# The embedding's product moved from the feed-forward stage to the start of a hybrid transformer layer, through memory

## The reference, cut to what matters

```
h   = layer_norm(x, ln_in_g, ln_in_b)
mix = hybrid_mixer(h, ...)                  # retention, gated delta rule, LRU, output product
h   = layer_norm(DN_ALPHA * h + mix, ln1_g, ln1_b)
ffn = moe(h, ...)                           # 64 experts, 8 per token, and one shared expert
ple = sigmoid(h @ ple_w_g + ple_b_g) * (p @ ple_w_e)      # p (1024, 256), ple_w_e (256, 1024)
out = layer_norm(DN_ALPHA * h + ffn + ple, ln2_g, ln2_b)
```

## Time and profile before

| what | value |
|---|---|
| median of 3 runs | 2537.09 us (2535.78 to 2537.4) |
| the profiled execution's own time | 2537.53 us |
| its span | 2535.4 us, 26796 instructions |
| mean granted clock of TensorE | 0.988 |
| PE matmul busy | 2438.1 us (96%), weight load 1478.4 us |
| DVE, ACT, POOL busy | 893.0, 437.6, 805.6 us |
| DMA | 391.37 MB, mean 154 GB/s |

### The profile page before, as it was taken

The page is one execution under the profiler, slowest core; times in us unless marked ns, Lnnn a source line. Parts: engine busy times, 40 slices in busy tenths (PEclk is TensorE's granted clock), DMA queues, the critical chain, the costliest instruction groups (busy, mean ns, idle before and its releaser), DMA issues. The chain is left out here.

```text
span 2535.4 us, 26796 instructions
## 1 busy us (share of the span) xinstructions
PE 2438.1 (96%) x10446; PEld 1478.4 (58%) x10446; DVE 893.0 (35%) x1522; ACT 437.6 (17%) x689; POOL 805.6 (32%) x764
## 2 busy tenths in 40 slices
PE   6999999999999999999999999999999999999992
PEld 3444554344699644444444544467777777787761
DVE  5010564575533523323223352222222223332224
ACT  1001122434454100100100110001111111111112
POOL 3000111011253100000001115436676666766654
PEclk9999999999999999999999999999999999999996
DMA  6201003100000211111142231269999999999995
GB/s 252 91 33 36 32 34 105 42 17 9 1 1 26 92 50 36 39 50 44 32 148 77 98 131 50 79 250 348 343 342 347 349 343 343 346 343 343 347 349 176
DMA packets 168141, 391.37 MB, mean 154 GB/s; under 512 B 19882, under 2 KB 40410, under 8 KB 167248
## 3 DMA queue, kind: packets, MB, share of 16 engines
q1 hardware_dynamic: 135424, 300.64, 32.6%
q0 software_dynamic: 31584, 82.00, 12.5%
q10 hardware_dynamic: 1008, 7.02, 0.7%
HBM read 322.50 MB, written 67.11 MB: 154 GB/s over the span
## 5 line engine op out<-in xcount | busy, mean ns | idle before, releaser
L1876 PEld LDWEIGHTS banks<-arena 128*128 128x128 f32 x4096 | 520.4, 191 | 58.0 <-issue 33.7
L1876 PE MATMUL banks<-arena 128*128 128x128 f32 (+7 forms) x4096 | 530.0, 290 | 13.5 <-DMA arena<-in_exp_w_gu 11.2
L2311 POOL DMA_INDIRECT arena<-hp_scratch,arena x306 | 295.0, 964 | 223.1 <-issue 80.0
L1380 PE MATMUL banks<-arena 128*128 128x512 f32 x672 | 293.4, 597 | 1.3 <-PEq L736 1.3
L328 PE MATMUL banks<-arena 128*128 128x512 f32 x640 | 280.9, 596 | 4.6 <-DVE arena L1093 4.3
L1884 PE MATMUL banks<-arena 128*128 128x512 f32 (+1 forms) x528 | 237.3, 592 | 1.3 <-DVE arena L2270 0.9
L1380 PEld LDWEIGHTS banks<-arena 128*128 128x128 f32 x672 | 128.3, 191 | 164.1 <-issue 163.9
L328 PEld LDWEIGHTS banks<-arena 128*128 128x128 f32 x640 | 120.0, 190 | 159.4 <-issue 149.7
L280 POOL TENSOR_SCALAR arena<-arena 128x1 f32<-128x1 f32 x16 | 15.5, 971 | 606.7 <-DVE arena L271 606.7
L2326 POOL DMA_INDIRECT acc_scratch<-arena x99 | 153.7, 1552 | 67.4 <-DMA acc_scratch<-arena 43.0
L321 PE MATMUL banks<-arena 128*128 128x512 f32 x384 | 168.1, 596 | 0.6 <-PE banks L321 0.6
(11 more groups left out here) (372 smaller groups left out, 2453.2 us busy)
## 6 DMA issues: line engine op xcount, KB each, us to landing
arena<-in_exp_w_gu SPq DMA_DIRECT2D x64, 2048.0 KB, 24.4
arena<-in_exp_w_down SPq DMA_DIRECT2D x64, 1024.0 KB, 20.5
arena<-in_w_in SPq DMA_DIRECT2D x10, 2048.0 KB, 9.0
arena<-in_w_in SPq DMA_DIRECT2D x12, 1024.0 KB, 6.1
arena<-in_w_branch SPq DMA_DIRECT2D x12, 512.0 KB, 7.1
hp_scratch<-arena SPq DMA_DIRECT2D x10, 512.0 KB, 2.7
acc_scratch<-arena SPq DMA_DIRECT2D x10, 512.0 KB, 4.0
arena<-hp_scratch,arena POOLq DMA_INDIRECT x306
```

Source lines behind the costliest of these rows:

```text
L1380: last = nc.tensor.matmul(PS[:, g % 4, :], lhs[:, k, :], rhs[:, k, :], start=(k == 0), stop=(k == 3))
L1876: last = nc.tensor.matmul(PS[:, bank + part, f * n:(f + 1) * n], weights[:, k, part * FF + f * P:part * FF + (f + 1) * P], x[:, k, 0:n], s ...
L2311: nc.gpsimd.indirect_dma_start(out=rows[0:n, :], out_offset=None, in_=table, in_offset=bass.IndirectOffsetOnAxis(ap=at, axis=0)).then_inc( ...
```

## The change

The product `p @ ple_w_e` is computed at the start of the first stage. SP loads `p` and `ple_w_e` ahead of x. TensorE turns `p` and makes the 16 pieces in banks 2 and 3 before its first `turn_tile`; ScalarE copies them into 16 buffers of SBUF. 13 of these lie in space that the retention uses later; three more, `p` and the weights lie where k and v will be written, so that VectorE waits for the stores before it evacuates job 8. SP stores the 16 pieces (256 KB each) into a new HBM tensor behind `h_scratch`. In the last stage the transposes and the product are gone; ScalarE's queue fetches the pieces into four buffers, four ahead at first and then one behind each sigmoid, three pieces ahead; VectorE multiplies by them from SBUF. The two loads of 1 MB leave that stage. SLOTS_AT goes from 9 to 12. `f_pl` counts one per piece instead of two.

```diff
-SLOTS_AT = 9
+SLOTS_AT = 12
...
+        e_d = nc.dram_tensor("embed_scratch", (P, NT, D), F32).ap()
...
+        take = lay(base + NT * W, base + 3 * NT * W)
+        p_in = take(NT * PLE).rearrange("p (t n) -> p t n", t=NT)
+        p_T = take(2 * SEQ).rearrange("p (f s) -> p f s", f=2)
+        p_we = take(2 * D).rearrange("p (f n) -> p f n", f=2)
+        p_out = [carve(HALF, R_RING + 2 * KD * W + 3 * W + i * HALF) for i in range(13)] + [take(HALF) for _ in range(3)]
...
             def _(sp):
+                sp.dma_start(p_in, a["p"].rearrange("(t p) n -> p t n", p=P)).then_inc(b_p, 16)
+                sp.dma_start(p_we, a["ple_w_e"].rearrange("(f p) n -> p f n", p=P)).then_inc(b_we, 16)
                 for i in range(2):
                     sp.dma_start(h[:, 2 * i:2 * i + 2, :], xv[:, 2 * i:2 * i + 2, :]).then_inc(a_x[i], 16)
...
                 sp.dma_start(h_d, h).then_inc(h_saved, 16)
+                sp.wait_ge(b_ev, 2 * NT)
+                for q in range(2 * NT):
+                    t, j = q // 2, q % 2
+                    sp.dma_start(e_d[:, t, j * HALF:(j + 1) * HALF], p_out[q]).then_inc(b_st, 16)
                 for g in range(2, 6):
...
                 pe.wait_ge(a_id, 16)
+                pe.wait_ge(b_p, 16)
+                for i in range(NT // 2):
+                    if i >= 2:
+                        pe.wait_ge(b_pT, i - 1)
+                    for c in range(4):
+                        last = nc.tensor.transpose(PS[:, 2 + i % 2, c * P:(c + 1) * P], p_in[:, 2 * i + c // 2, c % 2 * P:(c % 2 + 1) * P], ident)
+                    last.then_inc(b_tp, 1)
+                pe.wait_ge(b_we, 16)
+                pe.wait_ge(b_pT, NT // 2)
+                for q in range(2 * NT):
+                    t, j = q // 2, q % 2
+                    if q >= 2:
+                        pe.wait_ge(b_ev, q - 1)
+                    for f in range(2):
+                        last = nc.tensor.matmul(PS[:, 2 + q % 2, :], p_T[:, f, t * P:(t + 1) * P], p_we[:, f, j * HALF:(j + 1) * HALF],
+                                                start=(f == 0), stop=(f == 1))
+                    last.then_inc(b_em, 1)
                 turn_tile(0)
...
+                pe.wait_ge(b_ev, 2 * NT)
                 tile_in(0)
...
             def _(act):
...
+                for i in range(NT // 2):
+                    act.wait_ge(b_tp, i + 1)
+                    nc.scalar.activation(p_T[:, :, 2 * i * P:(2 * i + 2) * P].rearrange("p f (t s) -> p t f s", t=2),
+                                         PS[:, 2 + i % 2, :].rearrange("p (t f s) -> p t f s", t=2, f=2),
+                                         ACT.Copy).then_inc(b_pT, 1)
+                for q in range(2 * NT):
+                    act.wait_ge(b_em, q + 1)
+                    nc.scalar.activation(p_out[q], PS[:, 2 + q % 2, :], ACT.Copy).then_inc(b_ev, 1)
...
                 for job in range(NT - 3, 24):
+                    if job == NT:
+                        v.wait_ge(b_pT, NT // 2)
+                        v.wait_ge(b_em, 2 * NT)
+                        v.wait_ge(b_st, 32 * NT)
                     evacuate(job)
```

And in the last stage:

```diff
-                sp.dma_start(pt, a["p"].rearrange("(t p) n -> p t n", p=P)).then_inc(f_p, 16)
...
-                sp.wait_ge(f_hid, 4)
-                sp.dma_start(we, a["ple_w_e"].rearrange("(f p) n -> p f n", p=P)).then_inc(f_we, 16)
...
                     elif r == 1:
+                        sp.wait_ge(f_pl, NT)
+                    elif r < RING:
                         sp.wait_ge(f_pl, 2 * NT)
-                    elif r < RING:
-                        sp.wait_ge(f_pl, 4 * NT)
...
-                pe.wait_ge(f_p, 16)
-                pe.wait_ge(f_up, 3)
-                for t in range(0, NT, 2):
-                    if t >= 4:
-                        pe.wait_ge(f_pT, t // 2 - 1)
-                    for c in range(4):
-                        tt, f = t + c // 2, c % 2
-                        last = nc.tensor.transpose(PS[:, 4 + (t // 2) % 2, c * P:(c + 1) * P], pt[:, tt, f * P:(f + 1) * P], ident)
-                    last.then_inc(f_tp, 1)
...
-                    last.then_inc(f_pl, 1)
-                    if q == 0:
-                        pe.wait_ge(f_we, 16)
-                    for f in range(2):
-                        last = nc.tensor.matmul(PS[:, 4 + q % 2, :], pT[:, f, t * P:(t + 1) * P], we[:, f, j * HALF:(j + 1) * HALF],
-                                                start=(f == 0), stop=(f == 1))
                     last.then_inc(f_pl, 1)
                     if q == SLOTS_AT:
...
-                for i in range(NT // 2):
-                    act.wait_ge(f_tp, i + 1)
-                    nc.scalar.activation(pT[...], PS[:, 4 + i % 2, :]..., ACT.Copy).then_inc(f_pT, 1)
+                def embedded(q):
+                    j, t = q // NT, q % NT
+                    act.dma_start(em[q % 4], e_d[:, t, j * HALF:(j + 1) * HALF]).then_inc(f_em[q % 4], 16)
+
+                act.wait_ge(o_job, 2 * NT)
+                for q in range(4):
+                    embedded(q)
                 for q in range(2 * NT):
                     act.wait_ge(f_lg, q + 1)
                     nc.scalar.activation(pg[q % 2], pg[q % 2], ACT.Sigmoid).then_inc(f_sg, 1)
+                    if 1 <= q <= 2 * NT - 4:
+                        act.wait_ge(f_pr, q)
+                        embedded(q + 3)
...
-                    v.wait_ge(f_pl, 2 * q + 2)
+                    v.wait_ge(f_em[q % 4], 16 * (q // 4 + 1))
                     v.wait_ge(f_sg, q + 1)
-                    link(nc.vector.tensor_tensor(pg[q % 2], pg[q % 2], PS[:, 4 + q % 2, :], ALU.mult))
+                    link(nc.vector.tensor_tensor(pg[q % 2], pg[q % 2], em[q % 4], ALU.mult))
```

More of the change, by code:

```diff
@@ L303, in build @@
         a_id, a_gb, a_par, a_x, a_chain = sem("a_ident"), sem("a_gb"), sem("a_params"), [sem(f"a_x{i}") for i in range(4)], sem("a_chain")
+        b_p, b_we, b_tp, b_pT, b_em, b_ev = (sem("b_" + n) for n in ("p", "we", "tp", "pT", "em", "ev"))
+        b_st = sem("b_st")
         a_zero, a_pad = sem("a_zero"), sem("a_pad")
@@ L1526, in build @@
         slot_q = carve(4 * P, R2 + 2 * D + NT * 15)
-        we = carve(2 * D, R2).rearrange("p (f n) -> p f n", f=2)
         up = [carve(HALF, R2 + i * HALF) for i in range(2)]
@@ L1535, in build @@
         hid = take(2 * SEQ).rearrange("p (f s) -> p f s", f=2)
-        pt = take(NT * PLE).rearrange("p (t n) -> p t n", t=NT)
-        pT = take(2 * SEQ).rearrange("p (f s) -> p f s", f=2)
+        take(NT * PLE)
+        em = [take(HALF) for _ in range(4)]
         bg_row = take(D)
@@ L1577, in build @@
         e_slots = [sem(f"e_slots{i}") for i in range(2)]
-        f_w, f_p, f_bg, f_wg, f_we = (sem("f_" + n) for n in ("w", "p", "bg", "wg", "we"))
-        f_gu, f_sl, f_up, f_hid, f_dn, f_acc, f_tp, f_pT, f_pl, f_lg, f_sg, f_pr, f_chain, f_sl2, f_slq, f_stp, f_int = (
-            sem("f_" + n) for n in ("gu", "sl", "up", "hid", "dn", "acc", "tp", "pT", "pl", "lg", "sg", "pr", "chain",
+        f_w, f_bg, f_wg = (sem("f_" + n) for n in ("w", "bg", "wg"))
+        f_em = [sem(f"f_em{i}") for i in range(4)]
+        f_gu, f_sl, f_up, f_hid, f_dn, f_acc, f_pl, f_lg, f_sg, f_pr, f_chain, f_sl2, f_slq, f_stp, f_int = (
+            sem("f_" + n) for n in ("gu", "sl", "up", "hid", "dn", "acc", "pl", "lg", "sg", "pr", "chain",
                                     "slots_in", "slots_quad", "slots_t", "slots_int"))
@@ L1843, in _ @@
                     last.then_inc(f_dn, 1)
-                pe.wait_ge(f_pT, 4)
                 for q in range(2 * NT):
@@ L1983, in _ @@
                     nc.scalar.activation(up[q % 2], PS[:, 5 + 2 * (q % 2), :], ACT.Copy).then_inc(f_up, 1)
-                for i in range(NT // 2):
-                    act.wait_ge(f_tp, i + 1)
-                    nc.scalar.activation(pT[:, :, 2 * i * P:(2 * i + 2) * P].rearrange("p f (t s) -> p t f s", t=2),
-                                         PS[:, 4 + i % 2, :].rearrange("p (t f s) -> p t f s", t=2, f=2),
-                                         ACT.Copy).then_inc(f_pT, 1)
+                def embedded(q):
[4 more added lines that the diff above has]
+                    embedded(q)
                 for q in range(2 * NT):
@@ L2168, in ple_logits @@
                     j = q // NT
-                    v.wait_ge(f_pl, 2 * q + 1)
+                    v.wait_ge(f_pl, q + 1)
                     if q >= 2:
@@ L2243, in _ @@
                 gates_in(0)
-                v.wait_ge(f_pl, 4 * NT)
+                v.wait_ge(f_pl, 2 * NT)
                 for r in range(NS):
```

## The result

The kernel after takes **2542.12 us** (median of 20 runs, 2536.73 to 2550.31). The kernel before, in 20 runs beside them, takes 2537.31 (2535.78 to 2542.67). The ratio is 1.0021, with 1.0015 to 1.0026 as its interval: slower by 4.8 us, close to what can be told from no change, where I had forecast 4.4 us of gain. 2542.12 is outside my range. The profiled execution of after took 2542.1 us, its span 2540.2, which is 4.8 more than the 2535.4 of before. So the two profiles show the whole difference.

The account below looks back on a forecast made before the run. TensorE was taken to set the pace up to 2143 us, SP's weight queue behind it. Start +18.2 and last stage -22.6 gave -4.4 against 2537.53: 2533.1, as median 2532.7, with a range of 2526.5 to 2538.5.

Parts of the forecast that it names:

- The start: First stage: loads, transposes and product ahead of the first job cost 18.2 us, with bounds of 15.8 and 21.4.
- the slow clock: Start of TensorE's program: its rise from 1.2 to 2.4 GHz costs 1.0 us, 2.7 at most.
- The slots: Last stage: GpSimd's copy ends at 1622.0, set by 64 scatters; with SLOTS_AT 12 TensorE comes at 1629.2 without waiting.
- the fetches, costed at nothing: Loop of the last stage: 256 KB fetches on ACT's queue, three pieces (20 us) ahead, delay nothing but the next sigmoid.
- L1841's place and length: Last stage, shared expert's second product: without the transposes it can start at 1512.3 instead of 1512.85, gaining 0.55 us.
- wait ahead of `hidden(1)`: Last stage: place 1's gathers are ready at 1664.1, `hidden(0)` ends at 1660.4, so TensorE newly waits 3.7 us.
- The dear start: Rival: `p` at 8.5 and all of the slow clock (21.4 us), or later gathers: -1.2 to +1.9 us; chance 0.15.
- The stores: Start, SP's queue: 16 stores of 256 KB land at about 103, before VectorE's job 8 at 110.6; no wait.
- The rival of late stores: Stores of 2.7 us one after the other land at 134.5, TensorE stands 17 us before job 10: 2550; chance 0.06.
- The loop: Last stage: 16 pieces lose 1.72 us each, 27.5 us; pieces last 6.88, with VectorE and ScalarE under 3.5 us.
- what TensorE gains at 1680 is handed on whole: Experts: TensorE gives the pace up to 2143 and the weights follow, so its gain at 1680 passes on in full.
- the weights lead: Rival, experts: loads waiting for the loop's last matmul start 28.0 us earlier and set the end, gaining 9.8: 2527.3; chance 0.2.

Follow-up runs that it names:

- consts_late: Kernel after with ACT's 1.67 MB of constants issued behind the four copies of turned `p` instead of ahead; ratio 1.0003 to the kernel before.
- combined: Kernel after with ACT's constants issued behind the copies of `p` and slot indices made before the next piece's bias; 2534.04 us, ratio 0.9985.
- half8: Kernel after with only pieces 0 to 7 computed at the start, the rest in the loop, constants late, indices first, SLOTS_AT 11; 2532.05 us, ratio 0.9978.
- change_again: Kernel after, unedited, run on the second chip; 2538.85 us, ratio 1.0010 to the kernel before.
- no_fetch_again: Kernel after without the fetches of pieces 4 to 15, first four buffers reused, on the second chip; 2538.34 us, ratio 1.0005.
- late_alone: Kernel before's first stage with the change's last stage, fetches reading pieces of x and no embedding computed; 2614.85 us on the slower chip, ratio 0.996.
- no_fetch: Kernel after without the fetches of pieces 4 to 15, first four buffers reused; 2629.51 us on the slower chip, ratio 1.003.
- index_first: Kernel after with VectorE turning slots into indices before it waits for the next piece's bias; 2537.08 us, ratio 0.9999.
- start_alone: Kernel before plus the change's start (loads, product, stores, VectorE's waits), last stage unchanged; 2647.19 us on the slower chip, ratio 1.0095.
- quarter4: Kernel after with four pieces at the start, twelve in the loop, constants late, indices first, SLOTS_AT 10; 2531.68 us, ratio 0.9979.
- before_fetch: Kernel before plus sixteen unused 256 KB fetches of x on ACT's queue and VectorE's waits for them; 2548.14 us, ratio 1.0043.

## Why the prediction was wrong

Two steps failed. The start was mis-sized: 23.7 us instead of 18.2, since the weights were there at 16.3 and not by 11.9, `p` at 9.4 and not at 7.0, and the slow clock cost 2.5 us and not 1.0. The slots were taken to be out of reach of the change: the fetches, costed at nothing, made the scatters 8.8 us longer, and TensorE stood 2.80 us. Falls of the clock added 3.4 us that no term held.

Forecast: behind `hidden(1)` 4.4 us earlier. Measured: 7.3 later. The 11.7 us between them, in the order of time (the 25.8 us of 15 embeddings are the same on both sides):

| step | forecast | measured | difference |
|---|---|---|---|
| start, at the first bias | +18.2 | +23.66 | 5.5 |
| on the way to GpSimd's last shared product | 0 | -0.5 | -0.5 |
| L1841's place and length | -0.55 | +1.3 | 1.9 |
| wait at the slots | 0 | 2.80 | 2.8 |
| small pieces to `hidden(0)` | 0 | 0.2 | 0.2 |
| wait ahead of `hidden(1)` | 3.7 | 3.9 | 0.2 |
| its clock | 0 | 1.67 | 1.7 |

The fourth row holds the copy's delay; the measured value of the sixth is 1692.34 less the 7.14 us of `hidden(0)` and its start. The sum is 11.8, with rounding.

**The start** failed by its terms and not by its mechanism. "Its landing took 6.3 us in the last stage ...: 7.0 here" was priced by a row in which little else flowed. Here it was 9.38, even past my bound of 8.5. "The weights ... are there by 11.9 even if they only start then" was the worse step: they took 15.0 us and TensorE stood 3.19. For `p` I had sharing with ACT's queue as a bound, for the weights I had left it out; ACT's queue loads its constants at the same time, and in consts_late and combined, which move them back, the transposes start 2.4 us earlier and the first job 4.3 and 4.8. How much of `p`'s 2.4 us is the constants' is open, since half8 has them late too and got `p` at 8.83. The clock was 2.5 us instead of 1.0, near the 2.7 that I had as the most. The dear start that I gave as a rival, 21.4, was still 2.3 too cheap.

**The stores** were right: in time, no wait at job 8, and "I cost them at nothing" held, with 2 us of margin where the forecast had 7.6 (103 against 110.6). The rival of late stores, by which each would take 2.7 us one after the other, is refuted: sixteen were issued in 19.32 us and each landed after 8.6, so they overlap. By the Trainium skill, "DMA: Bandwidth & Descriptors", section on the anatomy of one DMA, 2.0 us plus bytes over 436 GB/s would be 2.6 us for each. The page states this for DMAs that GpSimd issues, and the stores are SP's; here they took 8.6 one beside another, and some 28 us for all instead of 42.

**L1841** was to gain 0.55 and lost 1.3. Its start gained 0.5 as forecast. But TensorE now stands 1.79 us for GpSimd, where the transposes of `p` had kept it busy, and the clock fell in the product behind it: 29.43 us for the same 64 matmuls. Eight traces have this wait, of 1.78 or 1.79 us: in five the product lasts 29.43 (after, consts_late, change_again, combined, no_fetch_again), in three 27.73 (late_alone, no_fetch, index_first). So a fall is not certain; what decides is open.

**The loop** was right: VectorE's biases are 6.88 us apart, and the 27.5 us are gone from it. VectorE and ScalarE had the time, and every fetch landed before its piece.

**The slots** were the step that failed by its mechanism: "GpSimd's copy of the slots ends at 1622.0, set by 64 scatters and not by TensorE". True, but not set by the scatters' count alone. The 256 KB fetches of ScalarE's queue run beside them and make the landings later. None of them, or only the first four: 97.8 to 100.9 us (before, start_alone, no_fetch twice). All sixteen, of which ten are issued while the scatters of after run: 106.9 to 113.7 in the six traces with the change's last stage. Half8 with eight has 106.6. Quarter4 has 104.3 with the first four alone, where no_fetch had 98.8 and 100.9; so some 4 us of these differences are not explained by the number of fetches. before_fetch shows that they suffice (109.6, TensorE 7.00 us), no_fetch that the lengthening goes with them (100.9, and 98.8 when repeated). I had costed the fetches by whether *they* were in time; whom they delay I had not asked. That they take engines or a queue from the scatters, and which, no run tells apart.

**The wait ahead of `hidden(1)`** was right in size and cause: 3.66 us against 3.7, and in change_again 2.27 plus the 1.6 by which a slow `hidden(0)` shortened it, for gathers that hang on piece 13. no_fetch_again keeps it, index_first takes it away. That 1.7 us of slow clock would come with it I had not seen; in change_again they fell into `hidden(0)`.

**The experts.** TensorE does lead, longer than before. But "what TensorE gains at 1680 is handed on whole" is only half true. In the table, with both marks equal (half8, quarter4, before_fetch), the last load follows them within 0.8 us. Where they differ, it comes out between them (index_first lies 0.3 beside): after has 0.0 and 7.3 and gets 4.0. Behind that load the span of no_fetch_again comes out 3.4 us better than its mark, which is not explained. The weights' stream, which starts when the loop ends, carries part of the time; the rival "the weights lead" had that part right. By it alone after would have had no loss at 2441. By the Trainium skill, the same page, section Specifications, the limit is about 358 GB/s; the experts run at 345 and 346 whether TensorE leads or the weights, and on the other chip at about 315, so the rate doesn't tell who leads. Nor is 358 a limit that every stretch here keeps: 415 GB/s flowed from 9.40 to 16.30 in after.

Why medians follow the spans only in part (half8: -9.9 us in the profile, -4.5 in the median; index_first -2.0 and +0.6) is in part open: the profiled executions of these two and of combined lie at the lower end of their runs, that of quarter4 (2531.68) is its median. Part of the spread goes with the clock: the three fastest executions of half8 (2527.33 to 2527.7) have a mean granted clock of 0.988, the other eight 0.986 or 0.987. I take the ratios as the measure and the profile for the places.

## What to carry to other kernels

Work moved into an idle stretch costs nothing only up to where the next stage could have started; here some 14 of 27.5 us nearly fitted (4.3 us paid), and half of the product moved brought `hidden(0)` 10.3 us forward, the whole with the same repairs 5.0. The medians of the two do not separate; against the whole as first written (ratio 1.0010) half is better clear of noise (0.9978). A transfer that is itself always in time is not free: look for the chain of small DMAs beside it, and for the other queues that load in the same microseconds. When a due time (`SLOTS_AT`) is shifted, look at what stands behind it in program order on the engine that delivers it: two lines exchanged on VectorE brought the gathers 7.0 us closer to the slots and took a wait of 2 to 4 us away.

## What the runs showed of the hardware

- Sixteen plain loads of 256 KB on ScalarE's queue, eight of them issued while it ran, made a chain of 64 small indirect scatters of GpSimd about 10 us longer (99.8 to 109.6 us in before_fetch). In after, 71 and 38 GB/s flow in the two slices of the page that hold the chain.
- TensorE's granted clock fell to 0.50 for about three microseconds after it had stood for only 1.79 or 3.66 us, and cost 1.7 us each. It fell behind the wait of 1.78 or 1.79 us in five of eight traces, and within `hidden(0)`, behind a wait of 2.03, in change_again; behind its wait of 2.27 it did not fall.
- 1 MB loads of the start landed after 8.5 and 15.0 us beside ACT's constants, and after 6.2 and 10.8 with these behind them (combined). In half8, which has them late too, the first took 8.0.
- On one of two chips the same kernel took 2621.94 us instead of 2537, all of it in the experts as far as start_alone's marks tell (`hidden(0)` at 1701.55, where the start's 22 us put it). In the profiles of late_alone, no_fetch and consts_late there `hidden(0)` was broken by gaps of 0.4 to 1.8 us at single matmuls, some 6.3 us in all, that nothing in the profile explains. In start_alone's, on the same chip, it was not.
